# Feed-forward up projections: one 512-column product over the high and low part of the input, a bank for each 128-wide block

## The reference

```python
# layers 0 and 1                          # layers 2 and 3
h = rms_norm(x, g) @ w_up                 gu = rms_norm(h, g) @ w_gate_up
y = conv_b + sum(conv_w[j] * h shifted    h = h + (silu(gu[:, :2816]) * gu[:, 2816:]) @ w_down
                 by 2 - j tokens, j < 3)
a, b = split(y)
x = x + (silu(a) * b) @ w_down
```

## Time and profile before

| | |
|---|---|
| median of 3 runs | 1512.74 us (1512.19 to 1512.75) |
| profiled execution, whole | 1512.45 us |
| its span, first to last instruction | 1510.6 us |
| TensorE busy | 1375.2 us (91%) |
| VectorE busy | 929.4 us (62%) |
| ScalarE busy | 678.3 us (45%) |
| mean granted TensorE clock | 0.949 |

### The profile page before, as it was taken

One profiled execution on the slowest core, in us unless ns is written; L12 is line 12 of the kernel. 1 busy time (PEld: TensorE's weight loads), 2 busy tenths in 40 slices (PEclk: granted clock), 3 DMA queues, 4 the chain that ended last, 5 costly groups with the idle time before them and its releaser, 6 DMA issues.

```text
span 1510.6 us, 23833 instructions
## 1 busy us (share of the span) xinstructions
PE 1375.2 (91%) x9801; PEld 1271.2 (84%) x9801; DVE 929.4 (62%) x1225; ACT 678.3 (45%) x848; POOL 20.3 (1%) x40
## 2 busy tenths in 40 slices
PE   6977999999994669689999899989999999999996
PEld 6977799999894666588999888789999888799996
DVE  4467467777767543457777766465655665565554
ACT  4335354444554321256444655463333554543332
POOL 3000000000000000010000000000000000000000
PEclk9889999999997876799999999999999999999998
DMA  9524046545551121054555443335555543365550
GB/s 303 180 81 143 29 146 208 177 167 198 164 168 56 56 73 40 29 182 140 184 202 194 137 146 118 134 113 196 194 185 178 166 140 124 120 206 181 193 186 37
DMA packets 175466, 221.74 MB, mean 147 GB/s; under 512 B 6240, under 2 KB 160192, under 8 KB 175264
## 3 DMA queue, kind: packets, MB, share of 16 engines
q1 hardware_dynamic: 172928, 215.55, 43.2%
q0 software_dynamic: 2128, 5.01, 1.0%
q10 hardware_dynamic: 336, 0.12, 0.0%
HBM read 219.60 MB, written 1.06 MB: 146 GB/s over the span
## 4 chain that ended last, share of the span: by engine, by line
PE 81%; DVE 9%; ACT 6%; issue 3%; DMA 0%; ACTq 0%; DVEq 0%
PE bank L341 24%; PE bank L343 23%; PE bank L342 23%; ACT whigh L1009 2%; DVE wlow L1344 2%; PE bank L789 2%; PE bank L579 1%; PE bank L415 1%; PE bank L619 1%; PE bank L823 1%; PE bank L605 1%; PE bank L828 1%; DVE score L1583 1%; DVE conv_b L1459 1%; ACT xs L1032 1%
## 5 line engine op out<-in xcount | busy, mean ns | idle before, releaser
L1344 DVE TENSOR_TENSOR wlow<-raw,whigh 128x2048 fp32r<-128x2048 f32 (+1 forms) x203 | 461.3, 2282 | 333.4 <-ACT whigh L1009 333.2
L1009 ACT ACTIVATE whigh<-raw 128x2048 fp32r<-128x2048 f32 (+1 forms) x203 | 384.5, 1904 | 441.6 <-PE bank L343 438.3
L341 PE MATMUL bank<-xn_high,whigh 128*128 128x256 f32 x1928 | 550.8, 286 | 6.8 <-issue 3.5
L342 PE MATMUL bank<-xn_low,whigh 128*128 128x256 f32 x1928 | 546.9, 284 | 0.0
L343 PE MATMUL bank<-xn_high,wlow 128*128 128x256 f32 x1928 | 546.9, 284 | 0.0
L341 PEld LDWEIGHTS bank<-xn_high,whigh 128*128 128x128 f32 x1928 | 371.2, 193 | 13.3 <-issue 7.8
L342 PEld LDWEIGHTS bank<-xn_low,whigh 128*128 128x128 f32 x1928 | 371.4, 193 | 1.4
L343 PEld LDWEIGHTS bank<-xn_high,wlow 128*128 128x128 f32 x1928 | 371.0, 192 | 0.0
L341 PE MATMUL bank<-whigh,g_high 128*128 128x512 f32 x352 | 139.3, 396 | 8.7 <-DVE y_low L1395 5.6
L342 PE MATMUL bank<-wlow,g_high 128*128 128x512 f32 x352 | 138.7, 394 | 0.0
L343 PE MATMUL bank<-whigh,g_low 128*128 128x512 f32 x352 | 138.4, 393 | 0.0
(11 more groups left out here) (260 smaller groups left out, 1503.5 us busy)
## 6 DMA issues: line engine op xcount, KB each, us to landing
raw<-in_ffn_w_up SPq DMA_DIRECT2D x44, 1024.0 KB, 5.2
raw<-in_w_gate_up SPq DMA_DIRECT2D x44, 1024.0 KB, 5.1
raw<-in_ffn_w_down SPq DMA_DIRECT2D x22, 1024.0 KB, 4.9
raw<-in_w_down SPq DMA_DIRECT2D x22, 1024.0 KB, 4.9
raw<-in_c_w_in SPq DMA_DIRECT2D x16, 1024.0 KB, 5.3
raw<-in_ab_w_in SPq DMA_DIRECT2D x14, 1024.0 KB, 5.3
raw<-in_w_in_fox SPq DMA_DIRECT2D x10, 1024.0 KB, 5.3
raw<-in_w_in_moba SPq DMA_DIRECT2D x10, 1024.0 KB, 5.3
```

The lines of the kernel that those rows point to most:

```text
L341: pe.matmul(o, lh, rh, start=start, stop=False)
L342: pe.matmul(o, lh, rl, start=False, stop=False)
L1009: act.activation(whigh[s][:, 0:w], raw[s][:, 0:w], ACT.Copy).then_inc(w_high, 1)
L1344: dve.tensor_tensor(wlow[s][:, 0:w], raw[s][:, 0:w], whigh[s][:, 0:w].bitcast(F), ALU.subtract).then_inc(w_low, 1)
```

## The change

`xn_high` and `xn_low` become two halves of one tensor, so that for each tile their 512 columns lie side by side. An up multiplies `whigh` with all 512 columns at once and `wlow` with the 256 columns of `xn_high`. The first product fills a whole bank: its left half takes high x high, its right half high x low; the second adds low x high to the left half. So each 128-wide block has a bank of its own, a uses banks 0 and 1, b uses 2 and 3, in every group, and the up waits for both of its banks before it starts. On the way out ScalarE copies the right halves to `rest_a` and `rest_b`, VectorE adds them to the left halves, and multiplies by `r` in a second instruction. The banks are empty after the sums. Who waited for a bank to be empty now waits for `up_ready`. `row_gain` is moved to make place for the two new tiles.

```diff
     def earlier(self):
-        return self.before if self.i is None else self.before + self.i
+        return self.before if self.i is None else self.i * 2 + self.before
...
-    xn_high, xn_low = at("xn_high", [P, KT, T], R), at("xn_low", [P, KT, T], R)
+    xn = at("xn", [P, KT, 2, T], R)
+    xn_high, xn_low = xn[:, :, 0, :], xn[:, :, 1, :]
...
-            def up(u, i, g, parity, a_or_b):
-                bank = 2 * parity + a_or_b
-                f, o = fill(("up", l, g, a_or_b), bank, i)
+            def up(u, i, g, a_or_b):
+                both = [fill(("up", l, g, a_or_b, j), 2 * a_or_b + j, i) for j in range(2)]
                 fetched(u, i, 6)
                 wh, wl = w_views(u, 256)
-                for j in range(2):
+                for j, (f, o) in enumerate(both):
                     for k in range(KT):
                         if i is None:
                             normed(j, k)
-                        last = split3(o[:, j * T:(j + 1) * T], wh[:, k, j * P:(j + 1) * P],
-                                      wl[:, k, j * P:(j + 1) * P], xn_high[:, k, :], xn_low[:, k, :],
-                                      k == 0, k == KT - 1)
-                last.then_inc(bank_full[bank], 1)
-                USED[u] = (bank_full[bank], f.before + 1, 1)
+                        c = slice(j * P, (j + 1) * P)
+                        pe.matmul(o[:, :], wh[:, k, c], xn[:, k, :, :].rearrange("p s t -> p (s t)"), start=k == 0, stop=False)
+                        last = pe.matmul(o[:, 0:T], wl[:, k, c], xn_high[:, k, :], start=False, stop=k == KT - 1)
+                    last.then_inc(bank_full[f.bank], 1)
+                USED[u] = (bank_full[f.bank], f.before + 1, 2)
...
 # ScalarE, ffn, group
-                act.wait_ge(bank_empty[fa.bank], fa.now)
-
                 if n > 1:
                     act.wait_ge(gate_ready, n - 1 if i is None else i * 2 + (n - 1))
+                for both, rest in ((fa, rest_a), (fb, rest_b)):
+                    for j, f in enumerate(both):
+                        act.wait_ge(bank_full[f.bank], f.now)
+                        last = act.activation(rest[:, j, :], psum[f.bank][:, T:2 * T], ACT.Copy)
+                    last.then_inc(rest_ready, 1)
+                act.wait_ge(up_ready, 2 * n - 1 if i is None else i * 4 + (2 * n - 1))
...
 # VectorE, ffn, group
-                for f, dst in ((fa, up_a), (fb, up_b)):
-                    dve.wait_ge(bank_full[f.bank], f.now)
-                    o = psum[f.bank][:, :].rearrange("p (j t) -> p j t", j=2)
-                    dve.tensor_tensor(dst[:, :, :], o, r, ALU.mult).then_inc(bank_empty[f.bank], 1)
+                for part, both, dst, rest in ((1, fa, up_a, rest_a), (2, fb, up_b, rest_b)):
+                    dve.wait_ge(rest_ready, 2 * n - 2 + part if i is None else i * 4 + (2 * n - 2 + part))
+                    for j, f in enumerate(both):
+                        dve.wait_ge(bank_full[f.bank], f.now)
+                        o = psum[f.bank]
+                        dve.tensor_tensor(dst[:, j, :], o[:, 0:T], rest[:, j, :], ALU.add).then_inc(bank_empty[f.bank], 1)
+                    dve.wait_ge(bank_empty[f.bank], f.now)
+                    dve.tensor_tensor(dst[:, :, :], dst[:, :, :], r, ALU.mult).then_inc(up_ready, 1)
```

More of the change, by code:

```diff
@@ L96, in earlier @@
     def earlier(self):
-        return self.before if self.i is None else self.before + self.i
+        return self.before if self.i is None else self.i * 2 + self.before
     @property
     def now(self):
-        return self.before + 1 if self.i is None else self.i + (self.before + 1)
+        return self.before + 1 if self.i is None else self.i * 2 + (self.before + 1)
 def build(nc, A, out, scratch):
@@ L149, in build @@
     up_a, up_b = at("up_a", [P, 2, T]), at("up_b", [P, 2, T])
+    rest_a, rest_b = at("rest_a", [P, 2, T]), at("rest_b", [P, 2, T])
     place[0] = ground
@@ L494, in down @@
                     USED[u] = (down_used, (GROUPS - 1) * l + g + 1, 2)
-            up(base, None, 0, 0, 0)
+            up(base, None, 0, 0)
             spread_rstd(n)
-            up(base + 1, None, 0, 0, 1)
-            up(base + 2, None, 1, 1, 0)
-            up(base + 3, None, 1, 1, 1)
+            up(base + 1, None, 0, 1)
+            up(base + 2, None, 1, 0)
+            up(base + 3, None, 1, 1)
             if l in MEMORY_NORM:
@@ L509, in ffn @@
                     u = base + 5 + 3 * j
-                    up(u, i, 2 + j, j, 0)
-                    up(u + 1, i, 2 + j, j, 1)
+                    up(u, i, 2 + j, 0)
+                    up(u + 1, i, 2 + j, 1)
                     down(u + 2, i, 1 + j, 1 - j, False, False)
             for b in range(4):
-                filled[b] += PAIRS - 1
+                filled[b] += 2 * (PAIRS - 1)
             g = GROUPS - 1
             u = base + 3 * g - 1
-            up(u, None, g, 0, 0)
-            up(u + 1, None, g, 0, 1)
+            up(u, None, g, 0)
+            up(u + 1, None, g, 1)
             down(u + 2, None, g - 1, 1, False, False)
@@ L1074, in group @@
                     high(a + 4, i)
-                fa, fb = FILLS["up", l, g, 0].of(i), FILLS["up", l, g, 1].of(i)
+                fa, fb = ([FILLS["up", l, g, part, j].of(i) for j in range(2)] for part in range(2))
                 n = GROUPS * l + g + 1
-                act.wait_ge(bank_empty[fa.bank], fa.now)
                 if n > 1:
                     act.wait_ge(gate_ready, n - 1 if i is None else i * 2 + (n - 1))
+                for both, rest in ((fa, rest_a), (fb, rest_b)):
[4 more added lines that the diff above has]
+                act.wait_ge(up_ready, 2 * n - 1 if i is None else i * 4 + (2 * n - 1))
                 if l < 2:
@@ L1084, in group @@
                         if part:
-                            act.wait_ge(bank_empty[f.bank], f.now)
+                            act.wait_ge(up_ready, 2 * n if i is None else i * 4 + 2 * n)
                         for j in range(2):
@@ L1450, in group @@
                         shift = 2 - tap
-                        for part, f, src, dst in ((0, fa, up_a, conv_a), (1, fb, up_b, conv_b2)):
+                        for part, src, dst in ((0, up_a, conv_a), (1, up_b, conv_b2)):
                             if tap == 1:
@@ L1470, in group @@
                     dve.wait_ge(silu_ready, n if i is None else i * 2 + n)
-                    dve.wait_ge(bank_empty[fb.bank], fb.now)
+                    dve.wait_ge(up_ready, 2 * n if i is None else i * 4 + 2 * n)
                     link(dve.tensor_tensor(gated[:, :, :], silu_a[:, :, :], up_b[:, :, :], ALU.mult))
```

4 lines of the change are left out of this document (2 added, 2 removed).

## The result

The changed kernel takes 1535.42 us (median; four executions from 1534.3 to 1536.75) where the one before takes 1512.53: a ratio of 1.0152, interval 1.0134 to 1.0169, or 22.9 us more. The forecast was slower, 1524.4, with a range up to 1535.0: the sign was right, the time lies 0.4 us above the range, and the loss is twice what was forecast.

What follows compares the result with a forecast made beforehand. TensorE was taken to bound the kernel (busy 91%, 81% of the chain). Saving -18.3, starts +18.0, ends +5.4 and clock +6.6 gave +11.7 us on 1512.45: 1524.2, stated as 1524.4 for the median, range 1516 to 1535.

Steps and rivals of the forecast that it cites:

- The saving of a block: In every up, three 256-column products become one of 512 and one of 256, saving 13 ns a block: -18.3 us.
- lower bound of 9.9 us: In the ups, if the 512-column product keeps 0.233 us in the mix, a pair saves only 7 ns: 9.9 us.
- The starts: Between groups 0 and 1 of each layer, pauses for shared banks, plus the first ups' waits: +18.0 us.
- The wait of the first up for the norm's low parts: In the first two layers the first up waits for low parts in banks 0 and 1: +0.6 us twice.
- The ends: At the last down of the first two layers, group 10's gate comes later: +2.7 us twice, +5.4 us.
- The seams of the loop: From down to up in the loops the evacuation is hidden: 0 us, upper bound 0.2 us at 36 seams.
- The clock: Low TensorE clock after the pauses at layer starts and the first two layers' ends: +6.6 us, between 0 and 13.
- The one with the unshortened clock (1517.8): At starts and ends the pauses come but TensorE restarts at 2.4 GHz: +5.1 us, 1517.8; chance 0.14.
- the one with stalls at the seams (1531.6): The loop's seams stall too, 0.2 us at each of 36, on top of the forecast: 1531.6 us; chance 0.17.
- The third, 2.5 ns a block and 1539: In the ups the joined product saves only 2.5 ns, 3.5 us instead of 18.3: 1539 us; chance 0.04.
- "Faster" at 26 ns a block: In the ups weight loads set the 256-column pitch, so a block saves 26 ns, 37 us in all: 1505.5; chance 0.05.
- No change: The starts are hidden better and the clock stays: within 0.2%, 1509.7 to 1515.8 us; chance 0.05.

Runs made afterwards that it cites:

- filled pause: The changed kernel with 20 unread 512-column products between group 0's second up and group 1's first up in each layer: 1526.71 us.
- widths in runs: Each block's 512-column products before its 256-column ones: on the changed kernel 1534.56 us; with early emptying and a later second-bank wait (the 0.37) 1506.5 us.
- the bank order alone: The kernel before, its products and evacuation kept, but every group uses bank 0 for a and bank 1 for b: 1538.65 us.
- the last group as before the change: The changed kernel with group 0 emptying its banks before the split, and group 10 of each layer in its old form: 1507.16 us.

## Why the prediction was right in its sign and wrong in its size

Both mechanisms of the loss were named rightly, and the loss was forecast 11 us too small because two terms were mis-sized, the saving of a block and the clock at the starts. By the forecast's own steps, on the same marks as the table above:

| us | forecast | measured |
|---|---|---|
| nine groups in four layers, gain | -15.0 | -9.0 |
| starts without the clock (pauses 18.0, less 3.3 gained in 16 ups) | +14.7 | +16.6 (filled pause) |
| last downs | +5.4 | +5.2 |
| clock, starts and ends | +6.6 | +9.6 |
| sum | +11.7 | +22.4 |

So of the 10.7 us missed the saving has 6.0 and the clock 3.0. The starts without the clock have 1.9, and the last downs 0.2 the other way.

*The saving of a block: the step that failed most.* The step was "From the two pitches that is 0.227 + 0.120 = 0.347 us", and with it 18.3 us. Both pitches were read in runs of one width. In alternation three blocks take 1.06 us in most groups and the pair 0.353; the loops' gain comes to 7.8 ns a block, which over all 1408 blocks would be an estimate of 11 us, against 13 ns and 18.3 us. My lower bound of 9.9 us named this case and I gave it no chance of its own, though the first pitches after a change of width, 0.24 at 1068.51 in the earlier trace rows, were the nearest row for a stream in which every pitch follows a change of width. Grouping the widths and moving the wait (16.61 us a group against 16.57) brought back nearly all of it in the loops, so there it is the order and not the products. The rule of the Trainium skill's page "TensorE: Matmul & The Clock Gate" (section "Back-to-back issue gap", 2.5 ns for each product, which the page gives for the isolated gap of one matmul) would have a group gain 0.08 us; the trace shows 0.25, and 0.37 with widths in runs, so it doesn't hold here.

*The starts: right.* Pauses of 5.25 us between the last product's due time and the next (5.2 forecast), in the place and by the mechanism named, with VectorE's `up_a` sum as releaser; the bank order alone gives them, and emptying before the split removes them. Two sums hold VectorE 0.75 us (0.76 forecast). The wait of the first up for the norm's low parts in both banks is there in the first two layers and nowhere else, 0.74 us each (0.6 forecast). From first up to first down the filled kernel is 14.0 us longer than the one before, where the forecast's steps give 13.5; the other 1.1 us of the 16.6 lie in stretches ahead of the ups that the change doesn't touch.

*The ends: right*, +2.56 and +2.58 against 2.7, b product and gate within 0.2 us of the forecast.

*The seams of the loop: right.* No bank wait there is in the list. The second `up_a` sum ends at least 0.28 us before the next up starts, in all four layers (0.29 forecast, of which 0.06 is the restart).

*The clock: right in kind, and the second step that failed in size.* The step was "I take 1.2 us for each of three starts, 0.6 for the second layer's and 1.2 for each end". The filled pause puts it at 8.7 us of time (9.6 on the marks) for the starts, where I had 4.2: 8.0 in the ups behind the pauses, since the clock stays low for 3.0 to 5.6 us of products, and 1.5 in the first layer's first up. Of the 2.4 us for the ends nothing could be shown. That the 2.4 us not found at the ends cover part of what the starts have in excess is luck.

*Rivals.* The one with the unshortened clock (1517.8) and the one with stalls at the seams (1531.6) are both out: the clock was low after every pause, and no seam waits. The third, 2.5 ns a block and 1539, is out by the pair of 0.352 on the mean (0.357 by that rival), though the measured time lies halfway between it and the second. "Faster" at 26 ns a block is out, since no group's mean pair fell under 0.347. (By the forecast's own sum it would have given 1506.1, not 1505.5, and 0.2% less time begins at 23 ns a block, not 22.) No change is out by the time.

Open: why the clock was low in the first layer's first up in the traces of three kernels (the changed one, widths in runs, the last group as before) and not in the others'. And what makes the pitches follow a three-block pattern in one group and not in the next. Both patterns occur in the same kernel in the same layer. I can only show that they vanish when the widths stand in runs or mirrored. And differences of 1 to 4 us between stretches that an edit doesn't touch keep single gains under some 2 us from showing in the time.

## What to carry to other kernels

Before a result is spread over more banks, follow each bank to its next writer at the edges of the loops too: inside the loop the down projection covered the evacuation with 0.2 to 0.3 us to spare, and where two groups have none between them the four starts paid 24 us, more than all that the edit could win. An engine that works in strict order should empty a bank before it takes up work that waits for a later matmul; here that reordering alone turned 1535.4 us into 1507.5. And price a mixed stream of instructions from rows where the kinds alternate, or take the lower bound as the likeliest value. The order that is best in a loop need not be best where the products wait for their input: the 512-column products in a run saved 2.8 us in the loops and cost 3.0 at the starts.

## What the runs showed of the hardware

Matmuls of 512 and 256 columns in alternation have pitches that cycle over three pairs (0.236, 0.113, 0.233, 0.117, 0.241, 0.120 us in the changed kernel's first layer, 1.060 in sum) or settle at 0.230 and 0.116; in runs they are 0.227 and 0.120. After a TensorE pause of 5.3 us the granted clock was 0.5 for 3.0 to 5.6 us, which cost the next up 1.4 to 2.5 us, and unread products in the pause gave that back.
